# A one-core encoder layer: another product order in the query/key projection, the first attention scores between its last two products, value rows asked for chunk by chunk

## The reference

```python
def parallel_mixer(hn, w_in, g_sgu_v, sgu_w, sgu_b, na_rpb, g_out_a, g_out_b, w_out):
    proj = hn @ w_in
    a = jax.nn.gelu(proj[..., :2 * D_SGU])
    y_a = spatial_gating(a, sgu_w, sgu_b, g_sgu_v)
    q, k, v = jnp.split(proj[..., 2 * D_SGU:], 3, axis=-1)
    y_b = neighbourhood_attention(q, k, v, na_rpb)      # softmax(q k * scale + bias) v in an 8 x 16 window
    y = jnp.concatenate([rmsnorm(y_a, g_out_a), rmsnorm(y_b, g_out_b)], axis=-1)
    return y @ w_out
```

## Time and profile before

| | before |
|---|---|
| median of 3 runs | 1222.16 us (1222.14 to 1222.35) |
| the profiled execution | 1222.25 us, its span 1220.4 us |
| PE busy | 1145.5 us, 94% of the span |
| DVE, ACT, POOL busy | 642.2, 469.8, 233.0 us |
| chain that ended last | PE 85%, DVE 4%, DMA 3%, issue 3%, ACT 2%, SPq 2%, POOL 1% |

### The profile page before, as it was taken

How to read it: one execution, slowest core, us unless ns; L and a number is a source line. 1 busy time by engine, 2 the same in 40 slices (tenths; PEclk the granted TensorE clock), 3 DMA queues, 4 the chain that set the end, 5 groups by cost and what they waited for, 6 DMA issues and landing times.

```text
span 1220.4 us, 18992 instructions
## 1 busy us (share of the span) xinstructions
PE 1145.5 (94%) x6854; PEld 916.9 (75%) x6854; DVE 642.2 (53%) x1244; ACT 469.8 (38%) x982; POOL 233.0 (19%) x337
## 2 busy tenths in 40 slices
PE   6999999999997999999999999999995999999956
PEld 5888888878884666888898788778784788887732
DVE  6332333212115897333465663754467998885256
ACT  6322333211005786111332433544323666674223
POOL 3322322200000000100100000100013333554344
PEclk9999999999997999999999999999996999999979
DMA  9573552834139424522221001912797999989967
GB/s 319 131 263 104 160 163 80 308 82 99 38 78 227 123 57 130 206 93 69 85 75 70 1 1 69 313 72 98 279 344 265 346 372 344 371 300 350 407 261 274
DMA packets 108427, 226.58 MB, mean 186 GB/s; under 512 B 28854, under 2 KB 48318, under 8 KB 108222
## 3 DMA queue, kind: packets, MB, share of 16 engines
q1 hardware_dynamic: 83822, 167.86, 40.6%
q0 software_dynamic: 17856, 43.02, 10.6%
q10 hardware_dynamic: 6672, 14.69, 3.8%
HBM read 180.89 MB, written 69.78 MB: 205 GB/s over the span
## 4 chain that ended last, share of the span: by engine, by line
PE 85%; DVE 4%; DMA 3%; issue 3%; ACT 2%; SPq 2%; POOL 1%; ACTq 0%; DVEq 0%; POOLq 0%
PE bank L570 18%; PE bank L572 18%; PE bank L571 18%; PE bank L2291 6%; PE bank L2219 3%; PE bank L2257 3%; PE bank L2089 3%; PE bank L2075 2%; PE bank L2064 2%; PE bank L2228 2%; PE bank L2153 1%; PE bank L2277 1%; DMA at<-v_att 1%; DVE at L565 1%; PE bank L1934 1%
## 5 line engine op out<-in xcount | busy, mean ns | idle before, releaser
L570 PE MATMUL bank<-at,at 128*128 128x512 f32 (+1 forms) x1192 | 442.4, 371 | 5.7 <-DVE at L565 2.5
L572 PE MATMUL bank<-at,at 128*128 128x512 f32 (+1 forms) x1192 | 432.1, 363 | 0.0
L571 PE MATMUL bank<-at,at 128*128 128x512 f32 (+1 forms) x1192 | 431.4, 362 | 0.0
L570 PEld LDWEIGHTS bank<-at,at 128*128 128x128 f32 x1192 | 226.4, 190 | 41.3 <-DVE at L565 3.3
L572 PEld LDWEIGHTS bank<-at,at 128*128 128x128 f32 x1192 | 225.9, 190 | 35.2
L571 PEld LDWEIGHTS bank<-at,at 128*128 128x128 f32 x1192 | 226.5, 190 | 32.5
L565 DVE TENSOR_TENSOR at<-at,at 128x1024 fp32r<-128x1024 f32 (+2 forms) x162 | 180.6, 1128 | 92.7 <-ACT at L560 90.2
L560 ACT ACTIVATE at<-at 128x1024 fp32r<-128x1024 f32 (+2 forms) x162 | 154.5, 988 | 163.4 <-DVE at L1510 51.4
L894 POOL TENSOR_TENSOR at<-at 128x1 f32<-128x1 f32 x88 | 23.7, 269 | 560.2 <-ACT at L1250 283.8
L2291 PE MATMUL bank<-at,at 128*128 128x512 f32 x156 | 74.2, 597 | 3.3 <-ACT at L1324 3.0
L990 POOL DMA_INDIRECT y_tok<-at,at x39 | 39.4, 1010 | 133.4 <-DVE at L1860 98.4
(11 more groups left out here) (213 smaller groups left out, 1351.0 us busy)
## 6 DMA issues: line engine op xcount, KB each, us to landing
at<-in_w_exp_gate SPq DMA_DIRECT2D x39, 512.0 KB
at<-in_w_exp_up SPq DMA_DIRECT2D x39, 512.0 KB
at<-in_w_exp_down SPq DMA_DIRECT2D x39, 512.0 KB
at<-y_tok SPq DMA_DIRECT2D x24, 512.0 KB, 9.7
at<-in_w_in SPq DMA_DIRECT2D x6, 1024.0 KB, 11.4
xT_hi_all<-at POOLq DMA_DIRECT2D x12, 512.0 KB, 3.9
xT_lo_all<-at POOLq DMA_DIRECT2D x12, 512.0 KB, 5.7
at<-xT_hi_all SPq DMA_DIRECT2D x3, 2048.0 KB, 10.3
```

What stands on the lines that cost most here:

```text
L570: nc.tensor.matmul(out, w_hi, x_hi, start=(k == 0), stop=False)
L571: nc.tensor.matmul(out, w_lo, x_hi, start=False, stop=False)
L572: last = nc.tensor.matmul(out, w_hi, x_lo, start=False, stop=(k == len(terms) - 1))
```

## The change

Four things are edited. (1) The last tile's att product goes to bank 7 and no longer waits for the copy of the tile before. (2) Pair 0 runs its six products as (tile, chunk) = (0,0), (1,0), (0,1), (0,2), (1,1), (1,2). (3) The last pair leaves the loop: its products run as (0,2), (0,1), (1,2), (0,0), (1,1), then the scores of step 0, then (1,0); the transposes of step 0 follow behind it, and DVE's and ACT's copies are reordered to match. `na_p` moves to the place of tile 0's weights, since tile 1's are still in use. (4) A new semaphore `chunk1_done` counts the last pair's chunk 1 products; SP asks for part 2 after the second one instead of after both `qk_done`. Part 0 and part 1 still wait for six `chunk2_done`, which now stand after the third product of the last pair.

```diff
-        na_p = [at(138 + 3 * j, 2, KREL * KC) for j in range(2)]
+        na_p = [at(kb, 2, KREL * KC) for kb in (132, 140)]
...
-            for j in range(2):
-                sp.wait_ge(qk_done[j], NH // 2)
+            sp.wait_ge(chunk1_done, 2)
             for n in range(4):
                 for r in range(QROWS):
                     sp.dma_start(*val_rows(2, n, r)).then_inc(vals_here[2], 16)
...
-                    act.wait_ge(qk_done[j], i + 1)
+                    if last:
+                        act.wait_ge(chunk1_done, j + 1)
+                    else:
+                        act.wait_ge(qk_done[j], i + 1)
                     nc.scalar.activation(*channel_chunk(2 * i + j, 1, bank[3 * j + 1][:]), ACT.Copy).then_inc(qk_evac_s[j], 1)
...
             def channel_tiles(i, last=False):
+                if last:
+                    for j in range(2):
+                        dve.wait_ge(chunk2_done, NH - 3 + j)
+                        nc.vector.tensor_copy(*channel_chunk(2 * i + j, 2, bank[3 * j + 2][:])).then_inc(qk_evac_v[j], 1)
+                    for j in range(2):
+                        dve.wait_ge(qk_done[j], i + 1)
+                        nc.vector.tensor_copy(*channel_chunk(2 * i + j, 0, bank[3 * j][:])).then_inc(qk_evac_v[j], 1)
+                        if j == 0:
+                            scores(0)
+                    return
...
                 if last:
-                    pe.wait_ge(att_copied, t)
-                    project(i, j, bank[4], 2, att_done)
+                    project(i, j, bank[7], 2, att_done)
...
-                    for n in range(NCH):
+                    for j, n in ((0, 0), (1, 0), (0, 1), (0, 2), (1, 1), (1, 2)):
                         pe.wait_ge(xT_here[n], 32)
...
+            def last_channel_tiles(i):
+                for j, n in ((0, 2), (0, 1), (1, 2), (0, 0), (1, 1), (1, 0)):
+                    if (j, n) == (1, 0):
+                        pe.wait_ge(qk_evac_v[0], NH)
+                        pe.wait_ge(qk_evac_s[0], NH // 2)
+                        scores(0)
+                    if n == 2:
+                        pe.wait_ge(lo_made, split_w_qk(i, j) + 1)
+                        pe.wait_ge(qk_evac_v[j], 2 * i)
+                        pe.wait_ge(qk_evac_s[j], i)
+                    channel_chunk(j, n, n == 0, then_values=True)
+
             channel_tiles(0)
-            with pe.Fori(1, NH // 2) as i:
+            with pe.Fori(1, NH // 2 - 1) as i:
                 channel_tiles(i)
...
-            for j in range(2):
-                pe.wait_ge(qk_evac_v[j], 2 * (NH // 2))
-                pe.wait_ge(qk_evac_s[j], NH // 2)
-            for s in range(N_STEPS + 2):
+            pe.wait_ge(qk_evac_v[1], NH - 1)
+            pe.wait_ge(qk_evac_s[1], NH // 2)
+            transpose_p(0)
+            pe.wait_ge(qk_evac_v[1], NH)
+            for s in range(1, N_STEPS + 2):
```

More of the change, by code:

```diff
@@ L1079, in _, with copy_att @@
                 split_w_in(2, half)
-            def copy_att(i, j):
+            def copy_att(i, j, last=False):
                 t = 2 * i + j
@@ L1084, in copy_att @@
                 act.wait_ge(v_stored[j], 16 * i)
-                nc.scalar.activation(v_st[j], bank[4][:], ACT.Copy).then_inc(att_copied, 1)
+                nc.scalar.activation(v_st[j], bank[7 if last else 4][:], ACT.Copy).then_inc(att_copied, 1)
                 act.wait_ge(att_copied, t + 1)
@@ L1092, in tile_work @@
                 if last:
-                    copy_att(i, j)
+                    copy_att(i, j, True)
                 elif is_first(i, j):
@@ L1457, in channel_tiles @@
                         nc.vector.tensor_copy(*channel_chunk(2 * i + j, n, bank[3 * j + n][:])).then_inc(qk_evac_v[j], 1)
-                    if not last:
-                        split_w(i + 1, j)
+                    split_w(i + 1, j)
             channel_tiles(0)
@@ L1522, in _ @@
             for s in range(N_STEPS + 2):
-                if s < N_STEPS:
+                if 0 < s < N_STEPS:
                     scores(s)
@@ L2015, in _, with channel_chunk @@
             tiles(pe, tile_work)
-            def channel_chunk(j, n, last):
+            def channel_chunk(j, n, last, then_values=False):
                 mm = split_products(bank[3 * j + n][:], [(w_qk_hi[j][:, k], w_qk_lo[j][:, k], xT_hi[n][:, k], xT_lo[n][:, k])
@@ L2023, in channel_chunk @@
                     mm.then_inc(chunk2_done, 1)
+                elif n == 1 and then_values:
+                    mm.then_inc(chunk1_done, 1)
             def channel_tiles(i):
@@ L2027, in channel_tiles @@
                     bank_free = {(0, 1): u_gelu, (1, 1): att_copied, (2, 0): v_gelu, (2, 1): mix_bias}
-                    for n in range(NCH):
+                    for j, n in ((0, 0), (1, 0), (0, 1), (0, 2), (1, 1), (1, 2)):
                         pe.wait_ge(xT_here[n], 32)
-                        for j in range(2):
[L2031 to L2035, removed]
+                        if n == 0:
+                            pe.wait_ge(lo_made, split_w_qk(0, j) + 1)
+                        if (n, j) in bank_free:
+                            pe.wait_ge(bank_free[n, j], NT)
+                        channel_chunk(j, n, n == NCH - 1)
                     return
@@ L2066, in scores @@
                             mm.then_inc(s_done, 1)
+            last_channel_tiles(NH // 2 - 1)
             def transpose_p(s):
@@ L2110, in _ @@
                     transpose_y(0, 0)
-                if 1 <= s <= N_STEPS:
+                if 2 <= s <= N_STEPS:
                     transpose_p(s - 1)
```

7 lines of the change are left out of this document (2 added, 5 removed).

## The result

| | before | after |
|---|---|---|
| first comparison, median of 6 runs each | 1222.15 us (1219.90 to 1223.24) | 1213.33 us (1212.56 to 1215.34) |
| ratio, 95% interval | | 0.9935, 0.9924 to 0.9945 |
| a later comparison, 11 and 6 runs | 1221.28 us (1219.15 to 1223.25) | 1214.62 us (1212.24 to 1217.68) |
| ratio, 95% interval | | 0.9945, 0.9929 to 0.9960 |
| profiled execution, its span | 1222.25 us, 1220.4 us | 1212.87 us, 1211.2 us |

The change makes the kernel faster: by 8.8 us in the first comparison and 6.7 us in the second by the medians, by 7.9 and 6.7 us by the ratios. One thing to keep in mind for all that follows: with more runs, before is not as steady as its first three times looked. Single times of either kernel spread over 3 to 5 us.

What follows compares the result with a forecast made beforehand. The chain is 85% PE, but before V0 the end is set by when the values are asked for. 1222.25 - 0.93 - 5.44 - 2.36 = 1213.5 us; range 1210.5 to 1216.4, held at 0.85 or so.

Steps and rivals of the forecast that it cites:

- Att into bank 7: Last tile: PE's 0.93 us wait before the att product goes and SP's bias requests move up as much; -0.93 us.
- The last pair's order: Last pair: value rows are asked for one product earlier and land as long after, so V0 comes sooner; -5.44 us.
- S0 between the last two products: End of last pair: step 0's scores move ahead of the last product, but V0 still waits for the values; 0.
- Pair 0's order: Pair 0: same six products, qk_done[0] raised earlier than needed, chunk 2 needed sooner with 2.9 us margin; 0.
- The clock held: V0 to V2: shorter PE stops keep the clock from falling; -2.36 us, bounds 0 and -2.36; chance 0.52.
- The gain passing to the end whole: Behind the attention: all work is started by the work before it, so the whole gain reaches the end.
- the sign of being wrong that I had named: Out projection behind the attention: the forecast is wrong if it starts with a wait that was not there.
- rival (d): Elsewhere, as before pair 1: other clock falls come or go, moving any case 1.5 us either way; no separate chance.
- The store: Step 4's output needs the first store, expected to land by 380.4; 0, or about 0.5 us late by ring order.
- Straight-line code (c): Unrolled last pair: fetching 144 matmuls once each slows PE; 1227.9 us at 0.1 us each; chance 0.03.
- V0 might wait for something else: At V0: the forecast is wrong if V0 waits for T1 or the exponentials instead of the values.

Runs made afterwards that it cites:

- the last two experiments: Two kernels built on the changed one, both asking for pair 1's first weights ahead of the bias requests, with two and then four output buffers: 1210.38 and 1207.19 us.
- the asking undone: Changed kernel, with value rows asked for as late as before (parts 0 and 1 after the last pair's fourth product, part 2 after the sixth): 1219.30 us, ratio 0.9984.
- att put back: Changed kernel with the last tile's att product back in bank 4 behind its wait: 1213.92 us, ratio 0.9949.
- att alone: Kernel before, with only the last tile's att product sent to bank 7: 1219.06 us, ratio 0.9989.
- the weights first: Pair 1's first weights asked for ahead of SP's first 28 bias requests, on top of the kernel of S1 first: 1210.38 us, ratio 0.9914.
- pair 0 put back: Changed kernel with pair 0's six products in the order of before: 1214.14 us, ratio 0.9941.
- S1 first: Changed kernel with part 1 of the value rows requested by SP, and step 1's scores also ahead of the last product: 1211.91 us, ratio 0.9920.
- four buffers: Four attention output buffers instead of two, on top of the kernel of the weights first: 1207.19 us, ratio 0.9883.

## Why the prediction was right, and where only its sum was

The forecast, 1213.5 us, is 0.2 from the first median and 1.1 from the second, and both lie in the range. Two of its three terms held in both traces of the changed kernel, with small losses; the third came by about a third in the first trace and whole in the second; and behind the attention both traces lose something that the forecast had at nothing.

**Att into bank 7, -0.93: right in mechanism, 0.63 in the first trace and 1.00 in the second.** In the first, SP's first bias request came 0.95 earlier; one request behind it took 0.32 longer. In the ten traces with this request in its old place (all but the last two experiments) it takes 0.85 to 1.24 us, so this is run to run. Undoing the edit moved V0 by 1.08.

**The last pair's order, -5.44: right, 5.06 and 5.14.** In the first trace SP asked 5.44 earlier in the clock-corrected count (357.21 less 0.63 and 1.58 is 355.00; it was 349.56), and V0 followed it 0.38 later than before. With the asking undone V0 moved back: at 376.41 it is 2.52 earlier than before, and 2.47 of this were gained by the end of pair 2, from att and from a fall before pair 1 that did not come. I had only assumed that the 21.5 us could be carried over; they are what parts 0 and 1 take when they share the DMA engines. Left to SP in turn, part 0 is in after 11.05 us.

**S0 between the last two products, 0: right.** Putting it behind moved V0 by 0.4, and the times are not told apart.

**Pair 0's order, 0: right.**

**The clock held, -2.36: a chance that I entered as a term.** I took a fall to be decided by how long PE stands still and how much work lies between. By the table that is not what decides. Before pair 1 the clock fell after stops of 1.81, 1.93, 1.95, 2.33 and 2.34 us and stayed full after 2.04, 2.09, 2.14, 2.25 and 2.29. In the cross-attention the stop is 2.04 in all twelve traces, and it fell in eight. The changed kernel, run twice, gave opposite answers at every place. What goes with the wait for the values is less: without one V0 to V2 took 3.81 or 3.82 in all five traces; behind waits of 3.5 us and more it took 5.0 to 6.3 in all three; behind waits of 0.6 to 1.0 it took 5.08 twice and 3.8 twice. So the chance to keep the clock looks better after the change, but it is a chance and no term. In the first trace V0 to V4 gained 0.86 instead of 2.36, in the second 2.35.

**The gain passing to the end whole: wrong in both traces.** The out projection gave back 0.74 us in the first and 1.00 in the second, in good part behind a y row load that was read 6.0 us after the asking instead of 4.5. This is close to the sign of being wrong that I had named, a wait there that was not there before. Between the attention and the cross-attention the traces of the experiments lose from nothing to 1.9 us (att put back); why that load comes late stays open.

**Other falls: rival (d), as described.** The two falls that were missing in the first trace, before pair 1 (1.58) and in the cross-attention (1.45), made up for what the three terms fell short, against a y row load that cost 0.74. Forecast terms: 0.63 + 5.06 + 0.86 = 6.55. The rest of the 9.38 is 1.58 + 1.45 - 0.74 and 0.54 from the routing stage, the last stages and what lies outside the span. In the second trace the terms give 8.49 of the forecast 8.73, no fall was missing, and 7.18 are left at the end. So the sum came near by two different ways, and that it is within 0.2 us of the first median is partly luck.

**The store, 0: right for the changed kernel, but by little, and not for the reason that I gave.** In the prediction the Trainium skill, page "DMA: Bandwidth & Descriptors", section "Queues, rings and completion order", stood against it: an engine consumes a queue's descriptors in ring order. By that rule the store lands behind part 2, and the traces agree. In all twelve the second of the first store's two DMAs lands 0.35 to 0.89 us after the last row of part 2, whether this is 3.1 us after its asking (att alone) or 5.7 (the last two kernels with the weights first); in the trace of before, where I had read 3.9 us as the store's own time, it lands at 388.26 and part 2 at 387.83. With the weights first, part 2 is in at 376.89 and the store, asked for from 370.94 on, at 377.38; DVE's scaling of step 4 starts at 377.90. As V0 moves up this becomes the wait that decides: PE lost 0.56 us at T7 with pair 0 put back, 2.14 with S1 first, 2.49 with the weights first, nothing with four buffers. In the changed kernel's first trace step 4 was scaled at 381.67, 0.89 after V4 began, as before; in the second, with the clock held, at 381.61, 1.19 after, and PE lost nothing by it. The trace with pair 0 put back, where the clock held too, lost about the 0.5 that the rule had given.

**Other rivals.** Straight-line code (c) cost nothing: the unrolled matmuls start 0.227 apart. That V0 might wait for something else is what the next experiments met, at T7.

What stays open: what decides whether the clock falls, since neither the length of the stop nor the program alone does; the runs here only show that it differs from run to run.

## What to carry to other kernels

Where PE waits for a transfer, ask for it one product earlier and count the gain nearly one for one (5.06 and 5.14 of 5.44 us here), but look first at what shares the DMA engines with it: here the same rows, asked for in the order of need by one queue, were in before any step stopped for them. When a consumer moves up by 3 us, follow every buffer behind it to the DMA that frees it; the two output buffers were enough only as long as V0 was late. And don't enter a fall of TensorE's clock behind a stop of some 2 us as a term; enter it as a chance, and take the stop itself away.

## What the runs showed that I had not expected

- The fall of the clock behind a stop is not a property of the program: the same stop of 2.04 us, in the same instructions, was followed by 1.2 GHz in eight traces of twelve. One such fall costs 1.2 to 1.6 us, and this is of the order of the spread of single times (1219.07 to 1222.89 us in 21 runs of before).
- A 2 MB gather by sixteen requests had its longest landing at 13.7 to 14.9 us beside an equal one in the eight traces of that kind. In the four traces with the requests in turn, the longest landing of the first 32 is 5.1 to 5.7 us.
- With S0 behind the last product one trace has a gap of 1.68 us in the middle of V4, between two halves that wait for nothing (379.42, eight matmuls; the next eight at 381.55, put down to issue). No other trace shows it there, and I did not find its cause.
